# Exponentials at the head of a differential step, rope sums and weight casts behind the coefficients, and POOL's low halves in two pieces

## The reference

```python
proj = jnp.einsum('bsd,de->bse', x, w_in[l])
...
ya = _stick_breaking_attention(qa, ka, va)          # 8 heads of 64
...
q1, q2 = _rope(qb[:, :, 0], cos, sin), _rope(qb[:, :, 1], cos, sin)
k1, k2 = _rope(kb[:, :, 0], cos, sin), _rope(kb[:, :, 1], cos, sin)
yb = _differential_attention(q1, q2, k1, k2, vb, lam)   # 4 heads, values of 128
...
# in _differential_attention, for a block of 128 queries and the keys up to its end:
    p1 = jax.nn.softmax(jnp.where(mask, z1, -jnp.inf), axis=-1)
    p2 = jax.nn.softmax(jnp.where(mask, z2, -jnp.inf), axis=-1)
    w = p1 - lam * p2
    outs.append(jnp.einsum('bhqk,bhkd->bhqd', w.astype(v.dtype), v[:, :, :end]))
```

## Time and profile before

| | us |
|---|---|
| median of three runs | 1521.79 |
| lowest, highest | 1521.19, 1521.81 |
| the profiled execution | 1519.07 |
| its span in the profile | 1516.9 |
| PE busy | 1475.1 (97%) |
| DVE busy | 1007.9 (66%) |
| ACT busy | 666.8 (44%) |
| POOL busy | 328.2 (22%) |

### The profile page before, as it was taken

The page is one execution under the profiler, slowest core; times in us unless marked ns, Lnnn a source line. Parts: engine busy times, 40 slices in busy tenths (PEclk is TensorE's granted clock), DMA queues, the critical chain, the costliest instruction groups (busy, mean ns, idle before and its releaser), DMA issues. The chain is left out here.

```text
span 1516.9 us, 19312 instructions
## 1 busy us (share of the span) xinstructions
PE 1475.1 (97%) x7152; PEld 1226.8 (81%) x7152; DVE 1007.9 (66%) x1232; ACT 666.8 (44%) x1035; POOL 328.2 (22%) x212
## 2 busy tenths in 40 slices
PE   8999999999999998999999999999999999999997
PEld 7788888887887787888787877888888888888886
DVE  3677877779866556553346688766665467668767
ACT  3455554546556555443021344444444344433343
POOL 2535444446432223210130140000000000000004
PEclk9999999999999999998999999999999999999999
DMA  5101112111110000110452233644442677935553
GB/s 177 56 29 57 56 43 70 55 55 56 43 57 28 29 14 28 39 48 12 136 183 107 89 110 116 217 153 153 153 153 97 215 275 256 325 137 194 194 196 137
DMA packets 111503, 172.40 MB, mean 114 GB/s; under 512 B 6080, under 2 KB 71616, under 8 KB 111296
## 3 DMA queue, kind: packets, MB, share of 16 engines
q1 hardware_dynamic: 111424, 171.33, 33.2%
HBM read 127.27 MB, written 44.04 MB: 113 GB/s over the span
## 5 line engine op out<-in xcount | busy, mean ns | idle before, releaser
L756 PE MATMUL p_proj<-xt_h,w_hi 128*128 128x512 f32 x640 | 254.6, 398 | 0.2 <-DVE xt_l L1589 0.2
L760 PE MATMUL p_proj<-xt_h,w_lo 128*128 128x512 f32 x640 | 253.5, 396 | 0.0
L758 PE MATMUL p_proj<-xt_l,w_hi 128*128 128x512 f32 x640 | 252.1, 394 | 0.0
L2265 POOL TENSOR_TENSOR w_lo<-w_raw,w_hi 128x1024 fp32r<-128x1024 f32 x48 | 120.4, 2508 | 240.2 <-DVE w_hi L1596 239.7
L760 PEld LDWEIGHTS p_proj<-xt_h,w_lo 128*128 128x128 f32 x640 | 120.8, 189 | 23.6
L756 PEld LDWEIGHTS p_proj<-xt_h,w_hi 128*128 128x128 f32 x640 | 120.8, 189 | 22.4 <-DVE xt_l L1589 0.6
L758 PEld LDWEIGHTS p_proj<-xt_l,w_hi 128*128 128x128 f32 x640 | 120.9, 189 | 20.7
L2378 POOL TENSOR_TENSOR row_odd<-row_odd,gains 128x1024 f32<-128x1024 f32 x4 | 10.4, 2622 | 580.7 <-ACT row_odd L1561 580.7
L1589 DVE TENSOR_TENSOR d_al<-f_a,d_ah 128x1024 fp32r<-128x1024 f32 x56 | 68.5, 1224 | 79.5 <-ACT d_ah L1479 79.5
L1479 ACT ACTIVATE d_ah<-f_a 128x1024 fp32r<-128x1024 f32 x56 | 59.2, 1057 | 134.0 <-PE p_av L1130 54.9
L1328 ACT ACTIVATE a_t<-p_tr 128x384 fp32r<-128x384 f32 (+3 forms) x96 | 47.2, 491 | 123.4 <-PE p_tr L858 123.3
(11 more groups left out here) (287 smaller groups left out, 3537.1 us busy)
## 6 DMA issues: line engine op xcount, KB each, us to landing
f_a<-h_terms SPq DMA_DIRECT2D x56, 512.0 KB, 3.4
w_raw<-w_in SPq DMA_DIRECT2D x40, 512.0 KB, 3.9
h_terms<-c SPq DMA_DIRECT2D x40, 512.0 KB, 3.2
f_b<-w_ff SPq DMA_DIRECT2D x40, 512.0 KB, 4.9
r<-w_ff SPq DMA_DIRECT2D x32, 512.0 KB, 4.0
gate_rows<-gst SPq DMA_DIRECT2D x12, 512.0 KB, 5.0
y<-x SPq DMA_DIRECT2D x8, 512.0 KB, 7.8
wo_raw<-w_out SPq DMA_DIRECT2D x8, 512.0 KB, 8.8
```

The source lines that it names most:

```text
L756: pe.matmul(o, w_hi[n_slot][:, k, :], xt_h[:, k, cols], start=(k == 0), stop=False)
L758: pe.matmul(o, w_hi[n_slot][:, k, :], xt_l[:, k, cols], start=False, stop=False)
L760: mm = pe.matmul(o, w_lo[n_slot][:, k, :], xt_h[:, k, cols], start=False, stop=(k == KT - 1))
L2265: pool.tensor_tensor(w_lo[slot][:, :, :], w_raw[:, :, :], w_hi[slot][:, :, :].bitcast(F32), ALU.subtract).then_inc(wt_lo, 1)
```

## The change

- ACT, differential groups: the exponentials that are due in a step come first in it, before the copy of the transposes and the copy of `p_av`.
- DVE, differential groups: a rope sum that was first in a step comes behind that step's coefficients and maxima; a cast of the weights that is due comes behind the coefficients and before the maxima, where it came at the step's end. In the stick-breaking groups both keep their places.
- POOL, everywhere: the low half of a tile of weights is made in two instructions of four of its eight rows each, and the low half of the keys in two of 512 tokens each, with one semaphore increment behind the second.

```diff
# ACT, attention(G), step k
+                    while scored:
+                        exponentials(*scored.pop(0))
                     act.wait_ge(tr_done, G.tr(k + 2) + 1)
                     at_free(act, G, k)
...
-                    else:
-
-                        while scored:
-                            exponentials(*scored.pop(0))
-                        if u + 2 < G.nunits:
-                            scored += [(u + 2, 0)] * (b == 0) + [(u + 2, 1)] * last_b
+                    elif u + 2 < G.nunits:
+                        scored += [(u + 2, 0)] * (b == 0) + [(u + 2, 1)] * last_b
# DVE, attention(G), step k
-                    if not G.sb and to_sum:
-                        rope_sum(*to_sum.pop())
...
                         if last_b and 0 < u < G.nunits - 1:
                             combine(u + 1)
+                        if tile_due is not None:
+                            split_next(tile_due)
                         if b == 0 and u + 2 < G.nunits:
                             peaks(u + 2, 0)
...
-                    due_before, tile_due = tile_due, tile_after(G, k)
-                    if G.sb:
-                        due_before, tile_due = tile_due, None
-                    if due_before is not None:
-                        split_next(due_before)
-                if tile_due is not None:
+                    tile_due = tile_after(G, k)
+                    if G.sb and tile_due is not None:
+                        split_next(tile_due)
+                if not G.sb and tile_due is not None:
                     split_next(tile_due)
# POOL, tile_low and low_keys
-                pool.tensor_tensor(w_lo[slot][:, :, :], w_raw[:, :, :], w_hi[slot][:, :, :].bitcast(F32),
-                                   ALU.subtract).then_inc(wt_lo, 1)
+                for ks in (slice(0, 4), slice(4, 8)):
+                    low = pool.tensor_tensor(w_lo[slot][:, ks, :], w_raw[:, ks, :], w_hi[slot][:, ks, :].bitcast(F32),
+                                             ALU.subtract)
+                low.then_inc(wt_lo, 1)
...
-                    pool.tensor_tensor(k_lo[m][r, :], stage[1][r, :], k_hi[m][r, :].bitcast(F32), ALU.subtract)\
-                        .then_inc(st_pool, 1)
+                    for cols in (slice(0, NH), slice(NH, S)):
+                        low = pool.tensor_tensor(k_lo[m][r, cols], stage[1][r, cols], k_hi[m][r, cols].bitcast(F32),
+                                                 ALU.subtract)
+                    low.then_inc(st_pool, 1)
```

## The result

The changed kernel takes **1504.49 us**, the median of four runs (1502.67 to 1505.31); the kernel before took 1521.49 beside it (four runs, 1519.31 to 1521.81). The ratio is 0.9892, 95% interval 0.9877 to 0.9907: 17.0 us less. In a later comparison it took 1505.41 against 1520.38, ratio 0.9906 (0.9889 to 0.9922): 15.0 us less. Its profiled execution took 1502.67 us, the span in the profile is 1500.6.

What follows compares the result with a forecast made beforehand. PE, busy 97% of the span, bounds the kernel; only its idle and low-clock time can be won. Terms -5.5 + 1.05 - 4.1 - 1.1 - 0.3 - 1.7 = -11.7 us; from the median 1521.79, forecast 1510.0, range 1506 to 1517.

Steps and rivals of the forecast that it cites:

- Exponentials first: Differential groups: PE's waits for ACT's exponentials in steps 4 and 3 go, step 1's grows; -5.5 us net.
- Step 1 grows: Groups 4 to 6: later rope sum delays swap copies, so PE's exponential wait grows +0.4 us each, +1.3 in all.
- Late copies: Steps 6 and 8, three groups: transposes' copies come behind exponentials and PE waits; +1.05 us.
- Rival 2: Late copies replace the removed waits, six tight places costing 1 us each; 1515 us, chance 0.13.
- rival 4: Slower: all copies go behind exponentials and the delay reaches PE; 1532 us at half of it, chance 0.05.
- Rival 3: Nothing shows: what is removed comes back at the chain's next link; about 1520 us, chance 0.07.
- Coefficients: PE's waits for DVE's coefficients, groups 4 to 7, fall from 6.4 to 2.3 us; -4.1, bounds -2.7 and -6.4.
- rival 1: POOL's second piece starts before waiting DVE is let in, so most of the pieces' gain goes; 1516 us, chance 0.13.
- The start: First scores: the second low query waits for one piece of the keys' low half, not a whole; -1.1 us.
- Stick-breaking groups: PE's 2.7 us of waits for split weights there change little; -0.3 us, bounds +2 and -1.5.
- The clock: The low-clock stretch from 543.6 to 547.1, after group 5's coefficient wait, stays away; -1.7 us, bounds 0 and +1.7.
- rival D: From the experiments: low-clock stretches come by themselves, whatever PE waits for; no chance given.

Runs made afterwards that it cites:

- clears added: Changed kernel plus two DVE clears of an unused buffer before the coefficients of unit 6 in groups 4 to 6; 1511.51 us against 1520.70, ratio 0.9945.
- sums at the head: Changed kernel with every rope sum of a differential step back at its step's head, casts still early; 1506.27 us against 1520.70, ratio 0.9904.
- padding: Changed kernel plus 14 more PE products of 256 columns before the very first scores, results overwritten; 1507.91 us against 1520.70, ratio 0.9916.

## Why the prediction was right or wrong

- **Exponentials first: right, a little too small.** Step 4: four waits gone (5.4 us), and the shift is 5.8; step 3: 1.4 forecast, 1.95 by the shift, since its waits were 0.4 to 0.5 each and the stretch gained 0.65. A wait that goes altogether gave 0 to 0.25 us more than its idle time; those that only became shorter gave about that. The prediction priced waits at their idle time.
- **Step 1 grows: right.** +0.4 each was forecast; it is +0.5, +0.3, +0.3. The mechanism is shown by the kernel with that sum at the head.
- **Late copies: too dear.** +1.05 us forecast, 0.45 found: step 8's copy follows the exponential at once (477.11, behind 1.12 us), and PE waits a few tenths. Rival 2 (1 us each) is refuted, and rival 4 (slower) with it: ACT's part alone is 11 us faster. Rival 3 (nothing shows) falls with the same run.
- **Coefficients: right.** The 896-wide ones take 1.69 us (1.8 forecast), the waits 1.9 in sum (2.3 forecast), 4.8 us by the shift against 4.1. What the prediction did not say is which part does it: the pieces alone bring 6.4 to 2.8, DVE's order alone to 4.1, and its lower bound, -2.7 without the pieces, is met at -2.6.
- **POOL's second piece: rival 1 is refuted.** DVE runs between the pieces, in the changed kernel and with the pieces alone. The Trainium skill (SBUF — State Buffer, Who interferes with whom) gives the shared pair for a whole instruction to whoever issues first. The trace agrees: the rope sum of 0.68 us took 0.82 when it met the first piece, ending 0.55 us after it, and 1.92 when it met a whole low half.
- **The start: half as forecast, and in another place.** PE's wait falls by 0.66 us (1.32 to 0.66), not by 1.1; that the shift there is -1.1 is luck, since 0.4 of it is the scatter before 15 us. The two queries take 4.43 us where they took 4.55, so the pieces of the weights do not shorten their wait as I had it; what gains is the cast ahead of them, which gets in between the keys' pieces.
- **Stick-breaking groups:** -0.6 against -0.3, all of it in group 3, which rotates tiles as well. POOL's additional work is hidden, as forecast, though it is 25 us and not 13: the 48 pairs for the weights cost 13.3 us more, 0.28 each, and the 16 for the keys 12.7, 0.79 each.
- **The clock: the step that failed.** The prediction says: "With half the idle gone I expect it to stay away: -1.7 us, bounds 0, and +1.7 if another comes. A longer low stretch in group 7's window (0.94 there) comes with the sums of squares, which the change leaves alone." It did stay away, but the term was mis-sized: over the runs, the clock gave 5.3 to 6.1 us, not 1.7, while the rest of the sum, forecast at 10.0, gave 10.9 to 11.8. Two errors are in the term. It took one profiled execution for all: that one lost 8.8 us to the low clock by the same count (half of 3.41, 10.24 and the 3.9 of the end), where the median run of that kernel lost 10.6 and took 2.4 to 2.7 us longer. And it took the stretch of the sums of squares as fixed, where it is 6.8 us long in ten of the fourteen profiles and 10.2 in four, once each in the two profiles of the kernel with step 0's sum at the head. No term was left for the clock to give more than the one stretch, so the range's good end fell short. Why the clock gave that much is not shown: that it follows PE's idle time is the likely part, below.

The sum, then, from the two profiled executions: -11.7 us forecast, -16.4 measured. Of the 4.7 us between, 1.5 are clock (3.2 by the shift against 1.7), 1.0 the waits of steps 3 and 4, 0.7 the coefficients, 0.6 the late copies, 0.3 the stick-breaking groups and 0.2 step 1; the rest is spread. So in this pair the clock is the largest miss of several, and over the runs it is most of the miss.

**What stays open:** why the sums of squares are slow for 6.8 us in one execution and for 10.2 in another, and how much of the difference between two kernels is that; and why one wait of PE is followed by a low stretch and a like one is not.

## What to carry to other kernels

Split a helper engine's long two-input instruction where an instruction that PE waits for is held off behind it: 25 us more of hidden work bought 5 to 12 us (by pairs of rows of the table that differ in POOL's part alone), and made a reordering of the other engine needless. Put ahead of a reordering the question of what the moved step releases (here a single swap buffer): moved behind the maxima the same rope sum paid in one step and cost in another. And where idle time of PE goes, leave room in the range for a gain of some us more than that idle time; read the granted clock of several runs before its term is written down, not that of one profile.

## What the runs showed of the hardware

Around PE's waits of two microseconds the clock can fall, not each time but in each kernel that has such waits in its differential groups. In groups 4 to 7 six kernels have a longest wait of 1.8 us or more: before (2.06), ACT's part alone (1.95), DVE's alone (2.90), no pieces (2.46), no ACT part (1.80), clears added (2.62). Each of the six profiles has one or two stretches at half clock there, and each begins between 0.6 us before the end of a wait of 1.7 to 2.8 us and 1.5 us behind it: 8 of the 18 waits of 1.6 us or more have one. In the eight profiles whose longest wait there is 1.4 us or less (the changed kernel twice, the one with step 0's sum at the head twice, pieces alone, sums at the head, no DVE part, padding) the groups have none but that of the sums of squares, which all fourteen have.

Behind the groups all fourteen profiles have one more long wait, of 2.8 us, that ends between 783 and 805 us, for which the trace shows no releaser. In three of them (pieces alone, no pieces, padding) a low stretch begins there, as in that of the padding, with the clock at 0.50 from 788.90 to 792.30:

```profile
789.10 0.77 PE L1032 MATMUL p_z<-wo_h,m_h 128*128 128x512 f32 x1 [2.82 <-issue]
```

So no low stretch of the fourteen traces, apart from those of the sums of squares and of the end, lies away from a wait of 1.6 us or more, and 11 of the 32 such waits have one (the time before PE's first product is not counted). This is a coincidence in place that rival D does not explain; how much time it is worth is not settled. Over all, the time lost to the low clock is 4.5 to 6.8 us at 16 to 20 us of PE idle time, 6.8 to 9.8 at 22 to 27, 10.6 at 28.9 and 13.0 at 33.2: some 0.4 to 0.5 us for each us of idle time from end to end. ACT's part alone, with three waits of 1.9 us, loses no more than the padding, whose longest in the groups is 1.4 (6.8 us each).

The Trainium skill (TensorE: Matmul & The Clock Gate, A second HAM failure mode) tells of a kernel in which short idles between groups of products are enough to make the clock swing, and says that this costs throughput. The rows here agree, with waits of 1.7 to 2.8 us. By the rule on an idle window that the prediction cited from the same page, the stretches beside these waits would not be there; the rows decide against it.

POOL's groups of instructions in the kernel after, count, busy us, mean ns, idle time before them:

```profile
L2262 POOL TENSOR_TENSOR w_lo<-w_raw,w_hi 128x512 fp32r<-128x512 f32 x96 | 133.7, 1414 | 223.1 <-DVE w_hi L1594 222.6 <-POOL k_lo L2284 0.3
L2284 POOL TENSOR_TENSOR k_lo<-stage,k_hi 64x512 fp32r<-64x512 f32 x32 | 58.3, 1841 | 18.5 <-DVE k_hi L1602 17.4 <-POOL k_lo L2284 0.6
```

Before, these were 48 of 2508 ns, 120.4 us, and 16 of 2850 ns, 45.6 us. A piece on half the partitions takes no less than one on all of them: both take 1.3 us where nothing holds them off (the keys' second piece from 43.10 on, the first piece of weights from 470.90 on). The keys' pieces are longer in the mean (1.84 us), as at 41.41 and 45.72 (1.73 and 1.74), where a cast or a low query of DVE runs beside them.
